# Two transformer blocks on one core: the mixer's branch products moved between the gate products

## The reference

```python
def swiglu(x, w_up, w_down):
    a, b = jnp.split(x @ w_up, 2, axis=-1)
    return (jax.nn.silu(a) * b) @ w_down          # hidden width 2816
...
    (sgu_u, sgu_v, ret_q, ret_k, ret_v, ret_g, pool_in,
     c_q, c_kv, k_rope, gate_logits) = _split(x @ w_in, IN_SIZES)
    ys = (sgu_mixer(...), retention_mixer(...), pool_mixer(...), mla_mixer(...))   # 256 wide each
    gates = jax.nn.sigmoid(gate_logits).reshape(bsz, seq, N_BRANCH, dm)            # 4 x 1024
    merged = gates[:, :, 0] * (ys[0] @ w_branch[0])
    for n in range(1, N_BRANCH):
        merged = merged + gates[:, :, n] * (ys[n] @ w_branch[n])
    return merged @ w_out
...
    for i in range(DEPTH_2):
        x = layer_norm(ALPHA * x + 0.5 * swiglu(x, ffn1_up[i], ffn1_down[i]), ln1_g[i], ln1_b[i])
        mix = token_mix(x, w_in[i], ...)
        x = layer_norm(ALPHA * x + mix, ln2_g[i], ln2_b[i])
        ple = jax.nn.sigmoid(x @ w_ple_gate[i]) * (p[i] @ w_ple[i])
        x = layer_norm(ALPHA * x + 0.5 * swiglu(x, ffn2_up[i], ffn2_down[i]) + ple, ln3_g[i], ln3_b[i])
```

## Time and profile before

| | us |
|---|---|
| runs of the kernel before | 1892.09 (1891.92 to 1907.99) |
| profiled execution | 1893.56 |
| its span | 1891.8 |
| PE busy in it | 1785.6 |
| DVE, ScalarE busy | 1088.6, 827.4 |

### The profile page before, as it was taken

The page is one execution under the profiler, slowest core; times in us unless marked ns, Lnnn a source line. Parts: engine busy times, 40 slices in busy tenths (PEclk is TensorE's granted clock), DMA queues, the critical chain, the costliest instruction groups (busy, mean ns, idle before and its releaser), DMA issues.

```text
span 1891.8 us, 22075 instructions
## 1 busy us (share of the span) xinstructions
PE 1785.6 (94%) x8840; PEld 1448.7 (77%) x8840; DVE 1088.6 (58%) x1602; ACT 827.4 (44%) x1181; POOL 93.0 (5%) x61
## 2 busy tenths in 40 slices
PE   7999969999999999999879999999999998799998
PEld 2878859897548878787768887788787877688876
DVE  3688536774525555655577554655456555775544
ACT  4444435423424443453725443344434537254442
POOL 0000054350000000000000000000000000000000
PEclk9999979988999999999889999999999998899999
DMA  8342510001246545544335554565455433355553
GB/s 331 135 154 100 190 23 2 2 1 45 90 138 251 181 175 179 199 170 142 112 112 206 194 179 174 181 223 195 156 180 198 172 140 112 112 205 195 180 173 115
DMA packets 41237, 284.80 MB, mean 151 GB/s; under 512 B 4400, under 2 KB 6576, under 8 KB 7728
## 3 DMA queue, kind: packets, MB, share of 16 engines
q1 hardware_dynamic: 39120, 268.61, 40.0%
q0 software_dynamic: 2016, 14.78, 2.0%
HBM read 282.32 MB, written 1.05 MB: 150 GB/s over the span
## 4 chain that ended last, share of the span: by engine, by line
PE 85%; DVE 8%; DMA 2%; ACT 2%; issue 2%; POOL 0%; SPq 0%; DVEq 0%; ACTq 0%; POOLq 0%
PE psum L409 80%; PE psum L412 5%; DMA ring<-stream 2%; DVE arena L1586 2%; DVE ring_lo L1592 1%; DVE arena L1589 1%; DVE sblk L1586 1%; ACT w_hi L1212 1%; DMA arena<-stream 1%; DVE arena L2027 0%; DVE arena L2024 0%; DVE small L2011 0%; DVE arena L2009 0%; POOL arena L1110 0%; DVE sblk L1655 0%
## 5 line engine op out<-in xcount | busy, mean ns | idle before, releaser
L1592 DVE TENSOR_TENSOR ring_lo<-ring,w_hi 128x1024 fp32r<-128x1024 f32 x416 | 490.3, 1222 | 317.2 <-ACT w_hi L1212 316.0
L1212 ACT ACTIVATE w_hi<-ring 128x1024 fp32r<-128x1024 f32 x416 | 416.4, 1052 | 419.2 <-DMA ring<-stream 304.6
L409 PE MATMUL psum<-w_hi,xT_hi 128*128 128x512 f32 (+1 forms) x1184 | 466.6, 394 | 8.5 <-DVE xT_lo L1592 6.0
L409 PE MATMUL psum<-w_hi,xT_lo 128*128 128x512 f32 (+1 forms) x1184 | 461.2, 390 | 0.0
L409 PE MATMUL psum<-ring_lo,xT_hi 128*128 128x512 f32 (+1 forms) x1184 | 460.9, 389 | 0.0
L409 PEld LDWEIGHTS psum<-w_hi,xT_hi 128*128 128x128 f32 x1184 | 224.8, 190 | 55.3 <-issue 8.8
L409 PEld LDWEIGHTS psum<-w_hi,xT_lo 128*128 128x128 f32 x1184 | 224.5, 190 | 46.5
L409 PEld LDWEIGHTS psum<-ring_lo,xT_hi 128*128 128x128 f32 x1184 | 224.9, 190 | 44.1
L1212 ACT ACTIVATE arena<-psum 128x512 f32<-128x512 f32 (+7 forms) x225 | 122.7, 573 | 252.8 <-PE psum L409 139.3
L409 PE MATMUL psum<-arena 128*128 128x64 f32 (+8 forms) x1480 | 192.9, 297 | 7.7 <-ACT arena L1212 5.9
L409 PEld LDWEIGHTS psum<-arena 128*128 128x128 f32 (+3 forms) x1480 | 169.2, 195 | 20.3 <-issue 7.4
(11 more groups left out here) (237 smaller groups left out, 1799.5 us busy)
## 6 DMA issues: line engine op xcount, KB each, us to landing
ring<-stream SPq DMA_DIRECT2D x249, 1024.0 KB, 4.8
arena<-ln_params POOLq DMA_DIRECT2D x6, 1024.0 KB, 6.5
arena<-par POOLq DMA_DIRECT2D x2, 1858.0 KB, 9.6
arena<-stream SPq DMA_DIRECT2D x3, 1024.0 KB, 6.9
ring<-rpb_bands SPq DMA_DIRECT2D x4, 512.0 KB, 6.8
cst<-const POOLq DMA_DIRECT2D x1, 1728.0 KB, 7.5
arena<-x_in POOLq DMA_DIRECT2D x1, 1024.0 KB, 12.5
arena<-ctx_in POOLq DMA_DIRECT2D x1, 1024.0 KB, 19.0
```

The costliest lines, as they stand in the source:

```text
L409: owe(nc.tensor.matmul(o, lhsT, rhs, start=first, stop=last), sem)
L1212: return A(o, i, ACT.Copy)
L1592: return V_.tensor_tensor(o, a, b, ALU.subtract)
```

## The change

Four things are changed in each of the two layers.

1. The branch products stand where their features are ready: product 0 (gating unit) behind gate block 4, product 1 (retention) behind block 6, products 2 (pool) and 3 (attention) behind block 7. The weight stream has the same order. All four heads' scores are computed before block 6, and `msc`, `mpT` and `mmx` have room for four heads. Attention's output goes to a place of its own (`y3`).
2. The gated sum is kept in the first gate's memory (`merged = gates[:, :, 0:D]`), and the output product waits for the merged features by pairs.
3. The down products wait for their hidden features by pairs, and the last transposes stand behind their first four blocks.
4. Slots 44 to 51 rotate over three high buffers; one slot split moves behind the norm of tile 0.

```diff
-            if 43 <= i < 58 or L == 0 and i < 2:
+            if 44 <= i < 52:
+                return (1, 3, 0)[(i - 44) % 3]
+            if 52 <= i < 57:
                 return i % 2
-            return (2, 3, 0, 1)[i % 4]
+            if L == 0 and i < 2:
+                return 1 - i
...
         mkT = carve(35008, 4, T)
-        msc = carve(V, 2, 384)
-        mpT = carve(V + 1024, 2, 384)
-        merged = carve(9728, 2, D)
+        msc = carve(V, 4, 384)
+        mpT = carve(V + 5632, 4, 384)
+        y3 = carve(V, 2, 256)
+        merged = gates[:, :, 0:D]
...
-            def split_gemm(name, hi, lo, tiles, nk, width=512, source=None, base=0, pairs=None):
+            def split_gemm(name, hi, lo, tiles, nk, width=512, source=None, base=0, pairs=None, between=None):
...
                 for k in range(nk):
+                    if between and k == 4:
+                        between()
                     if pairs and k % 2 == 0:
                         moved(pe, (pairs, k // 2))
                     for t, (o, sem) in zip(tiles, outs):
...
                                    pairs=f"xT{L}0" if f == 1 and cb == 0 else None)
                     if cb:
                         hidden(cb - 1)
-                hidden(FB - 1)
-                for cb in range(FB):
-                    moved(pe, (f"hT{L}{f}", cb))
                 w, done = source = split_chunks(hold=FB - 1)
-                split_gemm((f"down{L}{f}", 0), hfT_hi, hfT_lo, [0, 1], FK, 512, source)
+                split_gemm((f"down{L}{f}", 0), hfT_hi, hfT_lo, [0, 1], FK, 512, source, 0, f"hT{L}{f}",
+                           lambda: hidden(FB - 1))
...
                 split_gemm((f"g{L}", 4), xT_hi, xT_lo, [0, 1], KD)
-                split_gemm((f"g{L}", 5), xT_hi, xT_lo, [0, 1], KD)
+                def mixer_features(q, src):
+                    o, sem = open_bank((f"yT{L}", q))
+                    for j in range(2):
+                        for t in range(2):
+                            tr(o[:, (2 * j + t) * P:(2 * j + t + 1) * P], src[:, t, j * P:(j + 1) * P],
+                               sem if j and t else None)
+
+                def branch_product(n):
+                    moved(pe, (f"yT{L}", n))
+                    source = split_chunks()
+                    for cb in range(2):
+                        split_gemm((f"br{L}{n}", cb), yT_hi[:, 2 * n:2 * n + 2, :], yT_lo[:, 2 * n:2 * n + 2, :],
+                                   [0, 1], 2, 512, source, 2 * cb)
+                    source[1](((f"br{L}{n}", 1), 1))
+
+                pe.wait_ge(S(f"ysgu{L}"), 2)
+                mixer_features(0, yb[:, :, 0:256])
...
+                branch_product(0)
+                split_gemm((f"g{L}", 5), xT_hi, xT_lo, [0, 1], KD)
...
+                for h in range(4):
                     o, sem = open_bank((f"ms{L}", h))
                     mm(o[:, 0:P], mqT[0:96, h, 0:P], mkT[0:96, h, 0:P])
                     mm(o[:, P:384], mqT[0:96, h, P:T], mkT[0:96, h, :], sem=sem)
-
-                def mla_probs(h):
+                pe.wait_ge(S(f"yret{L}"), 2)
+                mixer_features(1, yb[:, :, 256:512])
+                for t in range(2):
+                    moved(pe, (f"py{L}", t))
+                mixer_features(2, yb[:, :, 512:768])
+                split_gemm((f"g{L}", 6), xT_hi, xT_lo, [0, 1], KD)
+                for h in range(4):
                     pe.wait_ge(S(f"mP{L}"), h + 1)
                     o, sem = open_bank((f"mpT{L}", h))
...
+                branch_product(1)
+                for h in range(4):
                     moved(pe, (f"mpT{L}", h))
...
                 split_gemm((f"g{L}", 7), xT_hi, xT_lo, [0, 1], KD)
+                for h in range(4):
+                    moved(pe, (f"mo{L}", h))
+                mixer_features(3, y3)
+                branch_product(2)
+                branch_product(3)
+                to_features(f"mgT{L}", lambda t, k: merged[:, t, k * P:(k + 1) * P], f"mg{L}")
+                split_gemm((f"wo{L}", 0), yT_hi, yT_lo, [0, 1], KD, pairs=f"mgT{L}")
...
-                    head(at + 13 + 2 * b)
+                    head(at + min(13 + 2 * b, 21))
...
                 gate(4)
-                gate(5)
                 for t in range(2):
                     root(f"gn{L}", t + 1, g4b[:, t, 0:4], g4[:, t, 0:4], eps5, 1.0 / 64)
+                evacuate_hi("yT", 0)
...
+                head(at + 23)
+                gate(5)
+                head(at + 24)
+                evacuate_hi("yT", 1)
+                evacuate_hi("yT", 2)
...
+                head(at + 26)
+                gate(6)
+                for h in range(4):
+                    evacuate((f"mpT{L}", h), mpT[:, h, :], lambda ps: ps[:, 0:384])
+                head(at + 29)
                 gate(7)
+                evacuate_hi("yT", 3)
+                head(at + 31)
+                for q in range(4):
+                    evacuate_hi("mgT", q)
                 head(at + 35)
...
                 residual(L, which, name, 0, 1, scale)
                 layer_norm(L, which, 0)
+                if nxt:
+                    part(ahead - 1)
                 residual(L, which, name, 1, 1, scale)
                 if nxt:
                     features_lo(*nxt, 0)
...
-                part(after)
                 last = f == 2 and L + 1 == LAYERS
+                part(after if last else after - 1)
...
+                def gated_branch(n, cb):
+                    for t in range(2):
+                        ps, free = take(dve, ((f"br{L}{n}", cb), t))
+                        gt = gates[:, t, n * 1024 + cb * 512:n * 1024 + (cb + 1) * 512]
+                        o = merged[:, t, cb * 512:(cb + 1) * 512]
+                        mul(gt, ps, gt).then_inc(free, 1)
+                        if n:
+                            moved(dve, ((f"br{L}{n}", cb), t))
+                            ins = add(o, o, gt)
+                            if n == 3:
+                                ins.then_inc(S(f"mg{L}"), 1)
+                            else:
+                                link(ins)
+
+                feature_lo("yT", 0)
...
+                    mul(y, y, prj[:, t, 1280:1536]).then_inc(S(f"yret{L}"), 1)
+                gated_branch(0, 0)
+                gated_branch(0, 1)
+                part(at + 23)
+                part(at + 24)
+                feature_lo("yT", 1)
+                feature_lo("yT", 2)
...
+                part(at + 26)
+                part(at + 27)
+                gated_branch(1, 0)
+                gated_branch(1, 1)
...
+                part(at + 29)
+                feature_lo("yT", 3)
+                gated_branch(2, 0)
+                gated_branch(2, 1)
+                part(at + 30)
+                gated_branch(3, 0)
+                feature_lo("mgT", 0)
+                feature_lo("mgT", 1)
+                gated_branch(3, 1)
+                part(at + 31)
+                feature_lo("mgT", 2)
+                feature_lo("mgT", 3)
                 part(at + 33)
...
+                   column_blocks(w[:, :2048]), w[:, 2048:2208],
+                   gate[:40], branch[0], gate[40:56], branch[1], gate[56:], branch[2], branch[3],
```

134 lines of the change are left out of this document (31 added, 103 removed).

## The result

The changed kernel took 1848.7 us (median of 4 runs, 1836.55 to 1858.17), the kernel before beside it 1900.0 us (1891.92 to 1910.59); the ratio is 0.974, interval 0.970 to 0.979. The forecast was 1852 us, range 1837 to 1870. Both kernels' times fall into two groups, 1837 to 1840 and 1856 to 1858 here, 1892 to 1893 and 1908 to 1911 before. The median of the first series lies between its groups.

The account below looks back on a forecast made before the run. TensorE, busy 94%, was taken to bound the kernel through its idle time and low clock. Mixer 22.4, third buffer 1.8, down products 15.3 and norms 1.5 sum to 41.0 us off 1893.56; forecast 1852 us, range 1837 to 1870.

Parts of the forecast that it names:

- Step 1: Behind gate block 4: a new PE wait of 1.8 us for pair 0's low part, plus 1.7 us for low clock.
- the third buffer's term: Gate blocks 1 to 4: an earlier slot copy removes block 2's wait, 0.9 us per layer, 1.8 in all.
- Steps 2 and 3: Blocks 5 to 7: block 5's split has 2.8 us of slack, PE has no wait, DVE waits some 3.5 us.
- Step 4: Mixer's tail: 10.0 us behind the branches, 2.2 of them transposes, so 7.8 us of idle remain where 11.6 were.
- the tail closes more: Mixer's tail: DVE runs ahead, half of 7.8 + 1.8 us disappears with its clock, 6.5 us per layer, 1839; chance 0.12.
- Step 5: Output product: the restart at low clock stays, 2.0 us.
- Down products: Start of the down products: four stops of 2.55 us go, 10.2, plus 5.1 of clock; 15.3 us in all.
- Norms: Split moved behind tile 0's norm: the stop only changes its releaser, 0.5 us three times, 1.5 in all.
- Late slots: Blocks 5 to 7 and branches: one weight slot late by 7.0 us once per layer, 1866; chance 0.18.
- Down gains nothing: Down products: third slot late, the stop only moves and the clock still falls, 15.3 us back, 1868; chance 0.05.
- Slower: Slot copies fall behind on ScalarE, six products wait, twice; 1918 at 5.5 us a product; chance 0.04.
- A long table switch: ScalarE on pair 0's path: switch takes twice the row's 1.28 us, +2.6 us, 1855; chance 0.03.

Follow-up runs that it names:

- the second series: The unchanged changed kernel measured again for its spread: 1839.4 us against 1892.8 for the kernel before, ratio 0.973.
- the run with pair 0 first: Changed kernel with ScalarE copying feature pair 0 ahead of the square root table switch and the two roots: 1835.9 us, ratio 0.970 to the kernel before.
- the other order: Changed kernel with both gated halves of branch 3 ahead of slot splits and merged low parts on DVE: 1826.8 us, ratio 0.966 to the kernel before.
- the old start: Changed kernel with all hidden-feature transposes and low-part waits again ahead of the down products' first matmul: 1857.0 us, ratio 0.981 to the kernel before.
- the kernel with two buffers and the clash: Changed kernel with blocks 1 to 4's slots on two high buffers, slots 51 and 52 both on buffer 0: 1858.1 us, ratio 0.983 to the kernel before.

## Why the prediction was right, by its steps

The time (1848.7 for 1852) came out nearer than its steps, and that is luck: the median lies between two groups, and the second series has 1839.4, just inside the range. The fairer comparison is 49.5 us against 41.0 from layer 0 on: the mixers gave 30.5 where 24.2 were forecast (22.4 and 1.8), the rest 18.9 for 16.8. The mechanism held, in its stops above all; what missed were sizes, most of them of the clock. Two slips in the working change little: the "five stops" of 16.1 us are six, and 1852.6 less 1.5 is 1851.

- **Step 1, the new stop behind block 4.** Forecast 1.8 us and 1.7 for the clock. It is 1.58 us and comes from the chain that was named; the run with pair 0 first shows it. The clock term did not come: PE goes on at 1.00 behind the stop in both layers. That is 1.7 of the miss in layer 0.
- **The start.** Block 4 starts 112.1 us behind the mixer's first matmul (885.53 - 773.39) where before it was 113.8 (876.40 - 762.56): 1.7 us earlier, of which the term for block 2 had 0.9. But the third buffer's term of 1.8 us for both layers is not all that it does. It was read from one stop of PE; in the new order slots that share a buffer can cost up to 10.7 us a mixer, of which the buffer's own part is not measured. The sum did not suffer, because the hand run had its copies in time already and so held the rest of the buffer's work under the mixer's 22.4.
- **Steps 2 and 3, blocks 5 to 7.** No stop, as forecast. DVE waited 3.5 us for block 7's second slot by the hand run; it waited 3.08, and 2.00 before that for the slots ahead of it (rows below). The four heads' output took 2.79 us and not 4.25. The price of 1.06 us a head came from the 52 records of the earlier trace rows, in which 12 wide matmuls were put at 2.1 us by the pitch of the split products. They are float32 products that aren't split: in the trace of before their starts lie 0.32 us (384 columns) and 0.43 us (512) apart at a clock of 1.00, 4.4 us in all, and the other 40 take 0.115 us each and not 0.18. 24 of those are 2.8 us. This made PE 1.5 us earlier than the path.

```profile
928.73 4.63 DVE L1598 TENSOR_TENSOR ring_lo<-ring,w_hi 128x1024 fp32r<-128x1024 f32 x4 [2.00 <-ACT w_hi L1220]
936.45 2.36 DVE L1598 TENSOR_TENSOR ring_lo<-ring,w_hi 128x1024 fp32r<-128x1024 f32 x2 [3.08 <-ACT w_hi L1220]
```

- **Step 4, the tail.** Forecast 10.0 us from the branches' end to the output product, of which 7.8 idle. It took 9.8 (963.49 to 973.28), with 2.07 + 4.13 = 6.20 idle and the transposes at low clock. The pieces were forecast as "3 + 4". The rival in which the tail closes more (6.5 us a layer) did not happen by itself; the other order brought part of it, 4.5 us in layer 0.
- **Step 5, the restart.** 12.82 us at 0.90 are 1.3 us, forecast 2.0.
- In all, layer 0's mixer gained 17.1 us and not 12.1: 1.7 for the clock behind block 4, 0.8 at the start, 1.5 for the heads' output, some 1.0 in small pieces that I did not follow. Layer 1's gained 13.4: it loses about 4.3 us to a low clock of which the next section speaks.
- **Down products.** Forecast 15.3, measured 17.9 and 19.7. The stops were right (4 x 2.55 = 10.2). The clock was the mis-sized part. I had 3 x 1.7; with the old start it fell behind all four, and the low stretch behind the last norm of layer 0 is 6.8 us instead of 3.4, another 1.7: 10.2 + 6.8 + 1.7 = 18.7 of the 19.7. By the two lowest times with the old start the clock's part can also stay away. The third slot had its slack: no stop inside the product.
- **Norms.** Forecast 0.5 each with a change of releaser; 0.3 to 0.4 each and one stop of 3.2 to 3.4 us for two.
- **The rivals.** Late slots: no PE stop by a slot at blocks 5 to 7. Down gains nothing: refuted. Slower: refuted; what came nearest to it is the kernel with two buffers and the clash, in which DVE's queue does back up behind a copy, and it is still faster than before (0.983). A long table switch: the rows below.

```profile
896.04 1.28 ACT L1499 ACTIVATE arena<-psum 128x512 f32<-128x512 f32 x2 [2.46 <-PE psum L414]
897.34 1.28 ACT L1422 ACT_TABLE_LOAD   x1
898.64 0.48 ACT L1422 ACTIVATE small<-small 128x4 f32<-128x4 f32 x2
899.03 0.57 ACT L1220 ACTIVATE yT_hi<-psum 128x512 fp32r<-128x512 f32 x1
```

The switch is on PE's path now, between the evacuation and the copy. It took 1.28 us, with 0.02 us on either side. The Trainium skill, "ScalarE: Activation LUTs", section "What ACT_TABLE_LOAD costs", puts a drain of about 1.38 us beside each switch; by an estimate from that figure the stop of 1.58 would have been near 3. This trace does not show the drain.

## What to carry to other kernels

When a stage is moved forward on the main engine, look for what stands in the helpers' queues between its inputs and their use: here one weight split that waited for a buffer held up a norm that needed no weights, at 10.7 us a mixer. A stop of the main engine doesn't price a buffer; what stands in the queue behind the blocked instruction has to be followed too. And when a buffer is taken away in a test, look at which neighbours share one at the seam of the rotation, or the test measures something else. Moving a split among the waits of one norm only deals the same 3.3 us out differently (it did change where the clock was low), while putting work that ends on the critical path ahead of work that doesn't (gating ahead of splits and low parts) gained 4.5 us a mixer at the cost of a line's place.
